# A two-layer block pair on one Trainium2 core: the first projection's weights in eight units of one row block, x in four pieces

## The reference, cut to what matters here

```python
proj = x @ w_in                  # x (256, 1024), w_in (1024, 8200)
mv   = proj[:, 4096:5120]        # the mLSTM values, 256 x 1024: first 512 columns, then the next 512
gate = proj[:, 6144:6152]        # its input and forget gates, 8 columns
mqk  = proj[:, 3072:4096]        # its queries and keys, before a causal convolution
```

## Time and profile before

| what | us |
|---|---|
| median of three runs | 1166.43 (1165.81 to 1166.51) |
| the profiled execution: its time | 1166.96 |
| the profiled execution: span of its trace | 1165.2 |
| PE busy | 1150.8, 99% |
| DVE busy | 772.8, 66% |
| ACT busy | 576.0, 49% |
| granted TensorE clock | 1.00 in every stretch of the first 40 us |

### The profile page before, as it was taken

The page is one execution under the profiler, slowest core; times in us unless marked ns, Lnnn a source line. Parts: engine busy times, 40 slices in busy tenths (PEclk is TensorE's granted clock), DMA queues, the critical chain, the costliest instruction groups (busy, mean ns, idle before and its releaser), DMA issues.

```text
span 1165.2 us, 18514 instructions
## 1 busy us (share of the span) xinstructions
PE 1150.8 (99%) x7762; PEld 1045.7 (90%) x7762; DVE 772.8 (66%) x1051; ACT 576.0 (49%) x663; POOL 27.9 (2%) x36
## 2 busy tenths in 40 slices
PE   8999999999999999999999999999999999999997
PEld 6989998998999988899998898899988789978996
DVE  4887856667655546697774667755555766875676
ACT  5565455442544434555544534444443456745663
POOL 0000000001000000000000000000000100010000
PEclk9999999999999999999999999999999999999999
DMA  9654454556665463645455556665666363346320
GB/s 340 225 201 160 149 202 163 192 180 201 224 210 189 165 208 128 236 161 181 140 185 182 178 184 217 218 204 181 192 200 216 137 217 128 126 151 238 120 99 37
DMA packets 129874, 211.62 MB, mean 182 GB/s; under 512 B 6528, under 2 KB 52608, under 8 KB 129664
## 3 DMA queue, kind: packets, MB, share of 16 engines
q1 hardware_dynamic: 128048, 204.15, 52.1%
q0 software_dynamic: 1744, 6.29, 1.8%
HBM read 209.37 MB, written 1.05 MB: 181 GB/s over the span
## 4 chain that ended last, share of the span: by engine, by line
PE 90%; DVE 4%; ACT 3%; issue 2%; DMA 1%; POOL 0%; SPq 0%; POOLq 0%; DVEq 0%; ACTq 0%
PE ps L500 88%; ACT wh L986 1%; DVE wl L1417 1%; PE ps L727 1%; DVE wl L1426 1%; DMA rv<-in_w_in 1%; DVE xl L1511 0%; PE ps L827 0%; ACT L1025 0%; PE ps L633 0%; DVE sg L1719 0%; ACT L1028 0%; DVE X L1692 0%; ACT ee L1304 0%; PE ps L809 0%
## 5 line engine op out<-in xcount | busy, mean ns | idle before, releaser
L1417 DVE TENSOR_TENSOR wl<-raw,wh 128x2048 fp32r<-128x2048 f32 (+1 forms) x185 | 414.9, 2248 | 170.1 <-ACT wh L986 169.8
L986 ACT ACTIVATE wh<-raw 128x2048 fp32r<-128x2048 f32 (+1 forms) x189 | 358.1, 1900 | 187.8 <-PE ps L500 165.3
L500 PE MATMUL ps<-xh,wh 128*128 128x256 f32 x1328 | 371.3, 280 | 0.9 <-issue 0.9
L500 PE MATMUL ps<-xl,wh 128*128 128x256 f32 x1328 | 368.1, 278 | 0.0
L500 PE MATMUL ps<-xh,wl 128*128 128x256 f32 x1312 | 364.3, 278 | 0.0
L500 PEld LDWEIGHTS ps<-xh,wh 128*128 128x128 f32 x1328 | 250.2, 188 | 4.0 <-issue 3.4
L500 PEld LDWEIGHTS ps<-xl,wh 128*128 128x128 f32 x1328 | 250.1, 188 | 0.2
L500 PEld LDWEIGHTS ps<-xh,wl 128*128 128x128 f32 x1312 | 246.6, 188 | 0.0
L500 PE MATMUL ps<-wh,xh 128*128 128x512 f32 (+1 forms) x440 | 172.2, 391 | 4.1 <-DVE xl L1511 2.0
L500 PE MATMUL ps<-wh,xl 128*128 128x512 f32 (+1 forms) x440 | 168.3, 382 | 0.0
L500 PE MATMUL ps<-wl,xh 128*128 128x512 f32 (+1 forms) x440 | 168.2, 382 | 0.0
(11 more groups left out here) (303 smaller groups left out, 1477.1 us busy)
## 6 DMA issues: line engine op xcount, KB each, us to landing
raw<-in_w_in SPq DMA_DIRECT2D x90, 1024.0 KB, 4.9
raw<-in_w_gate_up SPq DMA_DIRECT2D x88, 512.0 KB, 4.7
raw<-in_w_down SPq DMA_DIRECT2D x20, 1024.0 KB, 4.9
raw<-in_w_out SPq DMA_DIRECT2D x16, 1024.0 KB, 4.8
raw<-in_w_proj_ret SPq DMA_DIRECT2D x8, 1024.0 KB, 4.8
raw<-in_w_proj_mlstm SPq DMA_DIRECT2D x8, 1024.0 KB, 4.9
rows<-in_ln_g POOLq DMA_DIRECT2D x4, 512.0 KB, 4.2
rows<-in_ln_b POOLq DMA_DIRECT2D x4, 512.0 KB, 5.7
```

Of the source, the lines that this page charges most:

```text
L500: return pe.matmul(o, a, b, start=start, stop=False, skip_group_check=True)
L986: act.activation(stretch(wh, u, 0, m), source(u)[:, 0:m], ACT.Copy).then_inc(s_hi, 1)
L1417: dve.tensor_tensor(stretch(wl, u, a, nk * n), source(u)[:, a:nk * n], f32(stretch(wh, u, a, nk * n)), ALU.subtract).then_inc(s_lo, 1 if a ...
```

## The change

`mv0` comes as eight units of one row block (256 KB each; HEAD = 8), x as four pieces of two row blocks, ahead of units 0, 2, 4 and 6. `mv1` comes as three units of 2, 2 and 4 row blocks: units 8, 9 and 10. `gate` is unit 11, `mqk0` 12 and 13. `par` stands behind unit 10, `cst` behind unit 11. What PE computes, and in which order, is the same.

```diff
-HEAD = 5
+HEAD = 8
...
         if l == 0:
-            for k0, nk in ((0, 1), (1, 1), (2, 2), (4, 2), (6, 2)):
+            for k0, nk in ((0, 1), (1, 1), (2, 1), (3, 1), (4, 1), (5, 1), (6, 1), (7, 1)):
                 out.append((nk, 512, [(v[:, k0:k0 + nk, 4096:4608], 0, 512)], 0))
         else:
             cols(w, 4096, 512)
-        cols(w, 4608, 512)
+        if l == 0:
+            for k0, nk in ((0, 2), (2, 2), (4, 4)):
+                out.append((nk, 512, [(v[:, k0:k0 + nk, 4608:5120], 0, 512)], 0))
+        else:
+            cols(w, 4608, 512)
...
-FIRST = ((0, 2), (2, 2), (4, 4))
+FIRST = ((0, 2), (2, 2), (4, 2), (6, 2))
...
-        first = early[0][:, 0:512], early[0][:, 512:1024], early[0][:, 1024:2048], early[1][:, 0:1024], early[1][:, 1024:2048]
+        first = [early[u // 4][:, 512 * (u % 4):512 * (u % 4) + 512] for u in range(HEAD)]
...
-                if u in (0, 2, 3):
-                    q = max(u - 1, 0)
+                if u in (0, 2, 4, 6):
+                    q = u // 2
...
-                if u == 5:
+                if u == 10:
                     sp.dma_start(par[:, :, :], A["par"].rearrange("l p n -> p l n")).then_inc(s_par, 16)
-                if u == 7:
+                if u == 11:
                     sp.dma_start(cst[:, :], A["cst"]).then_inc(s_cst, 16)
...
-                act.activation(xh[:, k0:k0 + n, :], xT[:, k0:k0 + n, :], ACT.Copy).then_inc(s_xh, (1, 1, 2)[q])
-                highs((2, 3, 4)[q])
+                act.activation(xh[:, k0:k0 + n, :], xT[:, k0:k0 + n, :], ACT.Copy).then_inc(s_xh, 1)
+                highs(2 * q + 2)
```

More of the change, by code:

```diff
@@ L180, in tables @@
             at[name, l], n = n, n + 1
-            u += 1 if name == "gate" else 5 if (name, l) == ("mv0", 0) else 6 if name in ("dn0", "dn1") else 2
+            u += 1 if name == "gate" else HEAD if (name, l) == ("mv0", 0) else 3 if (name, l) == ("mv1", 0) else 6 if name in ("dn0", "dn1") else 2
             end[name, l] = u
@@ L324, in program @@
             sem(n) for n in ("s_cst", "s_par", "s_x", "s_warm", "s_gw", "s_row", "s_row2", "s_out", "s_last"))
-        s_xT = [sem(f"s_xT{q}") for q in range(3)]
+        s_xT = [sem(f"s_xT{q}") for q in range(len(FIRST))]
         s_xh, s_xl, s_xn, s_rm = sem("s_xh"), sem("s_xl"), sem("s_xn"), sem("s_rm")
@@ L436, in sync @@
                     sp.dma_start(dst[:, :, c0:c0 + w], src).then_inc(landed(u), 16)
-                if u == 5:
+                if u == 10:
                     sp.dma_start(par[:, :, :], A["par"].rearrange("l p n -> p l n")).then_inc(s_par, 16)
-                if u == 7:
+                if u == 11:
                     sp.dma_start(cst[:, :], A["cst"]).then_inc(s_cst, 16)
-                if u == 18:
+                if u == 22:
                     sp.dma_start(X[:, :, :], A["x"].rearrange("(t p) c -> p t c", p=P)).then_inc(s_x, 16)
@@ L493, in side @@
             def side(plan, steps, l, name, i):
-                for step in plan.get(name, ((),) * 12)[i]:
+                for step in plan.get(name, ((),) * 16)[i]:
                     kind, *at = step.split()
@@ L533, in ready @@
                     if v == 0:
-                        for q in range(3):
+                        for q in range(len(FIRST)):
                             if k == FIRST[q][0]:
-                                pe.wait_ge(s_xl, (1, 2, 4)[q])
+                                pe.wait_ge(s_xl, q + 1)
                     elif k % 4 == 0:
@@ L773, in tensor @@
                 if l == 0:
-                    one("mv0", xh, xl, xw, "tok", 5)
-                    one("mv1", xh, xl, xw, "tok")
+                    one("mv0", xh, xl, xw, "tok", HEAD)
+                    one("mv1", xh, xl, xw, "tok", 3)
                 else:
@@ L1198, in scalar @@
                     for c in range(2):
-                        one(f"mv{c}", lambda: [copy_mv(l, t, c) for t in range(2)], 2 if c else 5)
+                        one(f"mv{c}", lambda: [copy_mv(l, t, c) for t in range(2)], 3 if c else HEAD)
                     act.wait_ge(s_par, 16)
@@ L1864, in vector @@
             for q, (k0, n) in enumerate(FIRST):
[L1865 to L1868, removed]
+                dve.wait_ge(s_xh, q + 1)
+                dve.tensor_tensor(xl[:, k0:k0 + n, :], xT[:, k0:k0 + n, :], f32(xh[:, k0:k0 + n, :]), ALU.subtract).then_inc(s_xl, 1)
+                raise_high(2 * q + 2)
+                lows(2 * q + 2)
             steps = {
@@ L1879, in vector @@
                 if l == 0:
-                    one("mv0", lambda: mv_low(0, 0), 5)
-                    one("mv1")
+                    one("mv0", lambda: mv_low(0, 0), HEAD)
+                    one("mv1", None, 3)
                     before_layers()
```

## The result

| what | before, us | after, us |
|---|---|---|
| median of 20 runs each | 1166.21 (1165.58 to 1168.17) | 1168.76 (1167.40 to 1170.11) |
| the profiled execution: its time | 1166.96 | 1168.41 |
| the profiled execution: span | 1165.2 | 1166.6 |

The ratio after to before is 1.0020, with a 95% interval of 1.0014 to 1.0026: slower by 2.5 us, where 1.6 us faster was forecast. In the profiled pair the difference is 1.4 us. Reading the pair therefore explains 1.4; what makes it 2.5 in the medians is taken up with the runs.

The account below looks back on a forecast made before the run. PE, busy 99% of the span, could gain only at its waits before 11.29 and 33.69 us. 1.78 us won through mv1's start, less 0.19 before mqk0, gave 1.6: 1166.43 to 1164.8 us, range 1163.7 to 1166.7.

Parts of the forecast that it names:

- Part 1, the third row block earlier: Head of mv0: half of unit 2 lands at 8.19, so PE begins the third row block at 9.71, 1.58 us earlier.
- the rival of slow small transfers: At the head: 256 KB pieces take 2.25 us each, mv0 ends at about 28.5, time 1175; chance 0.02.
- Part 2, PE fed without a gap: mv0 and mv1: transfers, ACT and DVE keep ahead of PE, so gate ends at 31.03, 1.78 us earlier.
- Part 3, L + 3.99: Before mqk0: PE begins 3.99 us after unit 13 lands, at 32.1 instead of 33.69, 1.6 us earlier.
- L: Landing time of the second unit of mqk0, unit 13 after the change; forecast at 28.1 us.
- Part 3, "the deferral is hidden": Queue ahead of mqk0: gate and cst behind gate's wait still land by 22.55, with a tenth or two to spare.
- Rival 3: Gate and cst behind the wait let the queue run dry: L 30.8, mqk0 1.1 us later, 1167.5; chance 0.08.
- the old hold-up: In the kernel before, mqk0's first unit, then unit 8, landed at 27.1, held up by about 2 us.
- The sum, "which takes 0.19 back": Before mqk0: PE waits 1.07 us rather than 0.88, taking 0.19 off the 1.78 gain and leaving 1.6.
- rival 2: Before mqk0: L stays 29.0 to 29.8, PE waits 1.8 us longer, the gain is given back, 1166.2; chance 0.17.
- What is won reaches the end: After mqk0 begins: the other projections follow at the same distances, so what is won at 33.69 reaches the end.

## Why the prediction was wrong

**Part 1, the third row block earlier: right, and too low.** It begins at 8.95 rather than 9.71, with no wait. The reason is unit 1: it landed at 5.4 instead of 6.69, so that the second row block follows the first without the wait of 0.28 that it had the earlier trace rows, and begins at 7.59 instead of 8.19. I had carried that wait over from before unseen. In the second trace of after unit 1 landed at 5.95 and the third block is at 9.49, so this part varies by half a microsecond, and that the first trace beat the forecast by 0.76 was partly luck. No row showed the rival of slow small transfers: the pieces of 256 KB came some 0.65 us apart. (The fixed 2.0 us that the prediction gives beside the page's rule stand on that page of the Trainium skill in another section, "Anatomy of one DMA — SWDGE (gpsimd) path".)

**Part 2, PE fed without a gap: right.** No wait from the third row block to the end of gate. That end was forecast at 31.03 and came at 30.06, 2.75 us earlier than before; in the second trace it came at 30.76.

**Part 3, L + 3.99: right.** 29.11 + 3.98 = 33.09, and it held wherever the copies stood in their place, without a needless one, and waited for unit 13: 27.16 to 31.14, 27.56 to 31.55, 30.07 to 34.04, each within 0.03. With mv1 in two units it didn't (28.5 to 34.43), since PE itself ended mv1 late there, behind its wait and at half the clock. Reading the unnamed "issue" before mqk0 as the accumulators' copies was right too; in the trace after, the row names them.

**Part 3, "the deferral is hidden": wrong; this is the step that failed.** I had gate's landing fit the end of unit 10 and par with "a tenth or two to spare", by taking 18.2 for that end. In the first trace it was 17.1. gate went out at 15.70, also 0.9 earlier than I said, but landed 2.7 us later, not 2.1, at 18.4. cst landed at 23.0 rather than 22.55, unit 12 at 26.7 rather than 25.2, unit 13 at 29.1 rather than 28.1. In the second trace unit 10 and par ended at 18.0 and gate went out at 16.40, both nearly as forecast, and it was no better: gate landed 3.0 us later, at 19.4, cst at 23.65, L was 30.07. So the early end of the pieces ahead isn't the root, nor is gate's longer landing, for cst doesn't wait for it: its first bytes moved at 17.34 in the first trace, and gate landed at 18.4. What failed is the test. I compared landings, and a landing does not say until when the engines have work. This is the second trace in the microsecond before par landed:

```profile
17.00:18.00 1.00, 1.00 (x6) 0.84 (x5) 0.74 (x1) 0.29 (x1) 0.00 (x0) 1.00 0.47 68
```

Nor does a transfer move at its issue. Rows of 12.5 KB belong to cst alone. In the kernel before the first of them moves at 16.37, 1.8 us ahead of unit 6's landing at 18.16; in the two traces of after at 17.34 and 18.03, each 1.2 us behind cst's issue. That overlap is what the deferral took away. With cst issued early it is back (the first at 16.03), L is 27.56, and the median of 1165.65 lies inside my range. The rest of L's miss is a smaller term: from cst's landing to L I counted 5.55 us, and it took 6.1 and 6.4 in the two traces of after, 6.2 with cst early. Rival 3 named the mechanism, and the rates of 167 and 195 GB/s show it. But I tied it to L = 30.8, a gap and the old hold-up together, and let it decide only from L = 29.7 on.

**The sum, "which takes 0.19 back": wrong.** It prices PE's wait at its length. The wait became 3.03 us, and behind it half the clock cost 1.64 us more. No rival held this. Without it the profiled time would have been 1166.8, within 0.2 of before; in medians, by the run with seven needless matmuls, 1167.4, which is already 0.7 above my range, for the late landing and the term below. The wait could have been read ahead of time: rival 2 has it, 0.88 + 1.8 = 2.7 us, and I priced it at nothing but the lost gain.

**"What is won reaches the end": wrong by 0.38 us.** The loss at about 1047 us is in all eight profiled executions of kernels that have both parts, whatever their head looks like, also in the fastest ones, and in none of the other six. So it seems to belong to the program and not to the head's timing. DVE waits 2.54 instead of 2.19 there for a copy by ACT. What in the program makes it so I haven't tested.

**What stays open.** What decides whether the clock falls. It fell behind waits of 3.03, 3.78, 1.91 and 2.16 us, and it didn't behind waits of 3.29, 1.73 and 1.41 us, so the length alone doesn't decide. Then, whether the two groups of times in the kernels with a needless ACT copy are the clock or a held-up landing.

## What to carry to other kernels

A DMA issue that waits for a computing engine holds everything behind it on its queue, so put the large transfer that needs no wait ahead of it; here one line's place was worth 3.1 us, 1.55 of it in the landing and the rest by the lower clock behind the longer wait. Don't judge by landings whether the queue stays full: the engines can be nearly idle a microsecond before the last landing, and what is issued then takes another to move. And price a longer wait of PE not at its length alone: if PE reaches a late landing sooner, it only waits longer, and the clock may fall behind it and turn no gain into a loss.

## What the runs showed of the hardware that I had not expected

- The granted clock fell to 0.50 for about 3.4 us, after PE waits of 1.9 to 3.8 us, and the matmul pitch went from 0.12 to 0.21 us (256 columns) and from 0.23 to 0.43 (512). It began 0.6 to 1.4 us behind the restart of PE, not at it, and cost 1.6 us where I could compare the starts.
- It is a matter of the execution, not of the program alone: one program showed it in one trace and not in the other. The Trainium skill, page "TensorE: Matmul & The Clock Gate", section "What's actually happening", says that at a kernel's start the number of matmuls at the lower level differs from run to run of one kernel; here, in the midst of a kernel, it was the whole stretch that was there or not.
- The held-up landing of the first unit of mqk0 (27.0 to 27.1) came in both traces of before, with L at 29.7; in the traces of the same kernel with a needless ACT copy behind the split of that unit L is 28.2 and 28.4, though nothing ahead of the landing differs.
- A gate of 32 KB took 2.7 and 3.0 us to land in a queue that was nearly empty; one microsecond of such an empty queue is 0.4 MB at 402 GB/s.
- The engines ran out of work before the landings said so: 42 GB/s from 16.25 to 17.00 with landings at 16.8 and 17.1, and 68 GB/s from 17.00 to 18.00 with one at 18.0. The first bytes of cst moved 1.2 us behind its issue.
